# Moving the exchange of resident operands closer to their release in a Strassen-type matmul phase

## The reference

```python
def sq_relu_mlp(h, w1, w2):
    return jnp.square(jax.nn.relu(h @ w1)) @ w2

    x_lat = x_lat + m_lat[2] * y_lat          # y_lat ends in "@ w_out", 1024 x 1024
    h_lat = modulate(rms_norm(x_lat, norm2_g[l]), m_lat[3], m_lat[4])
    x_lat = x_lat + m_lat[5] * sq_relu_mlp(h_lat, w_mlp1[l], w_mlp2[l])   # 1024 x 4096, 4096 x 1024
return rms_norm(x_lat, final_g)
```

## Time and profile before

| | us |
|---|---|
| median of 3 runs | 3883.67 (3883.39 to 3904.89) |
| profiled execution, device time | 3888.39 |
| its span | 3886.6 |
| phase_out's products, first to last matmul | 2407.0 to 3873.8 |
| one f-unit or x-unit without exchange or turn | 19.04 |

### The profile page before, as it was taken

One profiled execution on the slowest core, in us unless ns is written; L12 is line 12 of the kernel. 1 busy time (PEld: TensorE's weight loads), 2 busy tenths in 40 slices (PEclk: granted clock), 3 DMA queues, 4 the chain that ended last, 5 costly groups with the idle time before them and its releaser, 6 DMA issues. The chain is left out here.

```text
span 3886.6 us, 98888 instructions
## 1 busy us (share of the span) xinstructions
PE 3376.4 (87%) x41417; PEld 2791.5 (72%) x41417; DVE 1966.0 (51%) x2884; ACT 1647.7 (42%) x2375; POOL 1668.3 (43%) x1364
## 2 busy tenths in 40 slices
PE   6899999999878888867777644989999999999998
PEld 3677888888767777756677513768877887777877
DVE  5488401110045555545555556564556546556575
ACT  5566313432145555532333412565555444323243
POOL 0220223222044545423555334545655665555554
PEclk7999999999989999985776766999999999999999
DMA  5133434453233333324343345676565557546453
GB/s 193 49 75 73 98 90 142 121 138 102 85 99 99 110 102 106 105 90 99 95 100 88 133 157 190 209 238 198 187 228 195 185 188 270 218 168 237 163 227 119
DMA packets 438927, 560.19 MB, mean 144 GB/s; under 512 B 119852, under 2 KB 355728, under 8 KB 413720
## 3 DMA queue, kind: packets, MB, share of 16 engines
q1 hardware_dynamic: 412704, 518.84, 41.8%
q10 hardware_dynamic: 20344, 21.04, 1.7%
q0 software_dynamic: 5632, 16.78, 1.5%
HBM read 354.42 MB, written 202.16 MB: 143 GB/s over the span
## 5 line engine op out<-in xcount | busy, mean ns | idle before, releaser
L2788 PE MATMUL o_pg<-o_t_hi,o_s_hi 128*128 128x512 f32 x2016 | 795.6, 395 | 62.7 <-DVE o_s_lo L2973 17.6
L2790 PE MATMUL o_pg<-o_t_lo,o_s_hi 128*128 128x512 f32 x2016 | 790.3, 392 | 0.0
L2791 PE MATMUL o_pg<-o_t_hi,o_s_lo 128*128 128x512 f32 x2016 | 789.8, 392 | 0.0
L601 PE MATMUL p_pg<-h_hi,p_whi 128*128 128x512 f32 (+1 forms) x1384 | 530.6, 383 | 9.6 <-DVE p_wlo L830 9.6
L601 PE MATMUL p_pg<-h_lo,p_whi 128*128 128x512 f32 (+1 forms) x1384 | 518.5, 375 | 0.0
L601 PE MATMUL p_pg<-h_hi,p_wlo 128*128 128x512 f32 (+1 forms) x1384 | 518.5, 375 | 0.0
L2788 PEld LDWEIGHTS o_pg<-o_t_hi,o_s_hi 128*128 128x128 f32 x2016 | 382.0, 189 | 157.8 <-issue 60.9
L2791 PEld LDWEIGHTS o_pg<-o_t_hi,o_s_lo 128*128 128x128 f32 x2016 | 381.9, 189 | 80.9
L2790 PEld LDWEIGHTS o_pg<-o_t_lo,o_s_hi 128*128 128x128 f32 x2016 | 382.5, 190 | 77.8
L2973 DVE TENSOR_TENSOR o_s_lo<-o_raw,o_s_hi 128x512 fp32r<-128x512 f32 x288 | 255.4, 887 | 209.3 <-ACT o_s_hi L2821 209.2
L601 PEld LDWEIGHTS p_pg<-h_hi,p_whi 128*128 128x128 f32 x1384 | 261.7, 189 | 61.0 <-DVE p_wlo L830 9.8
(11 more groups left out here) (330 smaller groups left out, 6625.1 us busy)
## 6 DMA issues: line engine op xcount, KB each, us to landing
o_raw<-in_w_mlp SPq DMA_DIRECT2D x32, 1024.0 KB, 5.9
scr_f<-o_xf SPq DMA_DIRECT2D x64, 512.0 KB, 7.7
o_raw<-scr_f SPq DMA_DIRECT2D x32, 1024.0 KB, 5.3
scr_w<-o_pre SPq DMA_DIRECT2D x16, 1792.0 KB, 6.5
o_t_raw<-scr_w SPq DMA_DIRECT2D x28, 1024.0 KB, 11.7
g_kqvb<-scr_kqv SPq DMA_DIRECT2D x72, 384.0 KB, 3.5
o_xf<-scr_x SPq DMA_DIRECT2D x22, 1024.0 KB, 7.9
p_raw<-in_w_in SPq DMA_DIRECT2D x38, 512.0 KB, 5.9
```

Of the source, the lines that this page charges most:

```text
L601: last = nc.tensor.matmul(pg[0:m, bank, 0:n], w[:, q, k, 0:m], h[bank][:, k, :], start=(k == 0 and j == 0), stop=(k == KT - 1 and j == 2))
L2788: nc.tensor.matmul(out, s_hi[:, q, k, :], t_hi[:, q, k, :], start=(not more and k == 0), stop=False, skip_group_check=more)
L2790: nc.tensor.matmul(out, s_hi[:, q, k, :], t_lo[:, q, k, :], start=False, stop=False, skip_group_check=more)
L2791: last = nc.tensor.matmul(out, s_lo[:, q, k, :], t_hi[:, q, k, :], start=False, stop=(k == 3), skip_group_check=more)
```

## The change

Eight edits in `phase_out`:

1. **Lag.** `T_HIGH` and `T_LOW` become 2 and 3: both splits of a resident part run one slot earlier in ScalarE's and VectorE's program. `prepared` and `LATE_PREP` say in which slot the next unit's stationary parts are prepared; with the values given each stays in its slot.
2. **Order of SyncE's queue at an exchange.** In the last unit `raw_load(i + 2)` stands ahead of `t_load` 0 instead of behind it. In the unit after, it moves to q = 1. For x-units the store of the unit before the last moves to q = 0 of the unit after, and the x tile that this unit needs is loaded one unit earlier (at q = 5 of the unit before the last). The x load of unit 40 moves from q = 2 to q = 5 of unit 39.
3. **Two turns by a diagonal.** For units 6 and 7 ScalarE doesn't scale x1 in place: it writes two 128 x 128 diagonals `diag` from the identity, and TensorE multiplies the unscaled tile by them (`matmul` in place of `transpose`). `scale` no longer waits for the store of x1, but for the turn before.
4. **`take_h(7)`** moves from slots (8, 5) and (8, 6) to (9, 2) and (9, 3).
5. **Joins.** For units 2 to 7, the pieces of the join of `h` move from two in slot 0 and two in slot 1 to one in slot 0, one in slot 1, two in slot 2. The last two joins move to slots 4 to 6 of units 8 and 9.
6. **`h_store`** moves from q = 2 to q = 3, for the last two blocks to q = 0 of units 9 and 10.
7. **`f_free`** waits for the store of x1 in the first two f-units.
8. The first load of `w_mlp2`'s preparation moves from slot 68 to slot 71.

```diff
--- before.py
+++ after.py
@@ -2297,10 +2297,11 @@
 UPB = 4
 PLAIN = {0: (0, 0), 2: (1, 0), 3: (0, 1), 5: (1, 1)}
 MIXED = {4: 0, 1: 1, 6: 2}
-PRE_AT = [68 + 13 * t for t in range(7)] + [171 + 13 * t for t in range(8)] + [281]
+PRE_AT = [71 + 13 * t for t in range(7)] + [171 + 13 * t for t in range(8)] + [281]
 PRE_PIECES = {3: (0, 1), 4: (2,), 5: (3, 4), 6: (5, 6), 7: (7,)}
 PRE_STORE = 9
-T_HIGH, T_LOW = 3, 4
+T_HIGH, T_LOW = 2, 3
+LATE_PREP = ((0,), (1,), (2,), (3,), (4,), (5,), (6,))
 
 
 def join_operands(eng, t, done, count):
@@ -2509,6 +2510,7 @@
         xf = sb("xf", [P, 2, 2 * D])
         pre = sb("pre", [P, 7, TB])
         ss, rs = sb("ss", [P, 2]), sb("rs", [P, 2])
+        diag = sb("diag", [P, 2, P])
         bank = ctx.enter_context(nc.psum_tensor("o_pg", [P, 4, TB], F32))
         pt = ctx.enter_context(nc.psum_tensor("o_pt", [P, 4, TB], F32))
         BX, BY, BV, BZ = range(4)
@@ -2532,6 +2534,14 @@
         N = M2 + FC * NW
         SETS = [0, M1, M1 + N1 // 2] + [M2 + NW * c for c in range(FC)]
         LAST_OF = {at - 1: k for k, at in enumerate(SETS) if k}
+
+        def prepared(i, q):
+
+            if i in LAST_OF:
+                return [(i + 1, q)]
+            if i - 1 in LAST_OF:
+                return [(i + 1, p) for p in LATE_PREP[q]]
+            return [(i + 1, q)] if i + 1 < N else []
 
         def is_x(i):
             return i < M1 or i >= M2
@@ -2672,20 +2682,29 @@
                 raw_load(1)
                 x_load(1)
                 for i in range(N + 2):
+                    last, first = i in LAST_OF, i - 1 in LAST_OF
                     for q in range(7):
-                        if i in LAST_OF:
+                        if q == (1 if first else 0) and i + 2 < N:
+                            raw_load(i + 2)
+                        if last:
                             t_load(LAST_OF[i], q)
-                        if q == 0:
-                            if i + 2 < N:
-                                raw_load(i + 2)
-                        if q == 1 and M1 <= i - 1 < N and not final_unit(i - 1):
+                        if q == 1 and M1 <= i - 1 < M2:
                             store(i - 1)
-                        if q == 2 and 0 <= i - 2 < M1:
+                        if not last and q == 1 and M2 <= i - 1 < N and not final_unit(i - 1):
+                            store(i - 1)
+                        if first and q == 0 and M2 <= i - 2:
+                            store(i - 2)
+                        if q == 3 and 0 <= i - 2 < M1 - 2:
                             h_store(i - 2)
+                        if q == 0 and M1 - 2 <= i - 3 < M1:
+                            h_store(i - 3)
                         if 7 * i + q - PRE_STORE in PRE_AT:
                             pre_store(PRE_AT.index(7 * i + q - PRE_STORE))
-                        if q == (5 if i + 1 == M2 + 2 else 2) and M2 <= i + 1 < N:
-                            x_load(i + 1)
+                        if M2 <= i + 1 < N and not (last and i >= M2):
+                            if q == (5 if i + 1 in (M2, M2 + 2) else 3 if first else 2):
+                                x_load(i + 1)
+                        if q == 5 and i + 1 in LAST_OF and i + 1 >= M2:
+                            x_load(i + 2)
                         if 7 * i + q in PRE_AT:
                             pre_load(PRE_AT.index(7 * i + q))
                         if q == 4 and final_unit(i - 1):
@@ -2798,8 +2817,11 @@
                         pe.wait_ge(h_taken, 8 * i)
                     for k in range(KT):
                         for m in range(2):
-                            last = nc.tensor.transpose(pt[:, k // 2, (k % 2 * 2 + m) * P:(k % 2 * 2 + m + 1) * P],
-                                                       x_tile(i)[:, m, k * P:(k + 1) * P], e.ident)
+                            to, tile = pt[:, k // 2, (k % 2 * 2 + m) * P:(k % 2 * 2 + m + 1) * P], x_tile(i)[:, m, k * P:(k + 1) * P]
+                            if i < M1 - 2:
+                                last = nc.tensor.transpose(to, tile, e.ident)
+                            else:
+                                last = nc.tensor.matmul(to, tile, diag[:, m, :], start=True, stop=True)
                     last.then_inc(turned, 1)
 
                 for i in range(N + 1):
@@ -2837,6 +2859,7 @@
                         eng.wait_ge(f_out[n % 2], 32 * (n // 2))
                     else:
                         eng.wait_ge(turned, NW - 1 + n)
+                        eng.wait_ge(x1_out[n], 16 * (NW // 2))
 
                 def rectify(i, k, src, to):
                     n = 3 * (i - M1) + k - 1
@@ -2879,6 +2902,11 @@
 
                 def scale(i):
                     act.wait_ge(inv, i + 1)
+                    if i >= M1 - 2:
+                        act.wait_ge(turned, i)
+                        for m in range(2):
+                            nc.scalar.activation(diag[:, m, :], e.ident, ACT.Copy, scale=rs[:, m:m + 1]).then_inc(scaled, 1)
+                        return
                     act.wait_ge(x1_out[i % 2], 16 * (i // 2 + 1))
                     for m in range(2):
                         t = x_tile(i)[:, m, :]
@@ -2907,8 +2935,8 @@
                                 take_p1(i)
                             if not is_x(i):
                                 f_unit(i, q)
-                        if i + 1 < N:
-                            s_high(i + 1, q)
+                        for at in prepared(i, q):
+                            s_high(*at)
                         if exchange(i, q, T_HIGH):
                             t_high(*exchange(i, q, T_HIGH))
                         if 0 <= i - 1 < M1 or final_unit(i - 1):
@@ -2921,8 +2949,10 @@
                         if 0 <= i - 1 < M1:
                             if q == 3:
                                 scale(i - 1)
-                            if q >= 5:
+                            if q >= 5 and i - 1 < M1 - 1:
                                 take_h(i - 1, q - 5)
+                        if i - 1 == M1 and 2 <= q <= 3:
+                            take_h(i - 2, q - 2)
 
             @block.vector
             def _(dve):
@@ -2932,6 +2962,7 @@
                         dve.wait_ge(f_out[n % 2], 32 * (n // 2))
                     else:
                         dve.wait_ge(turned, NW - 1 + n)
+                        dve.wait_ge(x1_out[n], 16 * (NW // 2))
 
                 def place(i, which):
 
@@ -2993,18 +3024,23 @@
                     for q in range(7):
                         if 0 <= i < N and q:
                             combine(i, q)
-                        if i + 1 < N:
-                            s_low(i + 1, q)
+                        for at in prepared(i, q):
+                            s_low(*at)
                         if exchange(i, q, T_LOW):
                             t_low(*exchange(i, q, T_LOW))
                         if (0 <= i - 1 < M1 or final_unit(i - 1)) and q == 2:
                             inverse(i - 1)
                         if final_unit(i - 1) and q == 3:
                             finish(i - 1)
-                        if 0 <= i - 2 < M1 and q < 2:
+                        if 0 <= i - 2 < M1 - 2 and q < 3:
                             if q == 0:
                                 dve.wait_ge(h_taken, 8 * (i - 1))
-                            for k in (2 * q, 2 * q + 1):
+                            for k in ((0,), (1,), (2, 3))[q]:
+                                join_piece(dve, lambda n: pre[:, n, :], k, h_joined, 4 * (i - 2))
+                        if M1 - 2 <= i - 2 < M1 and q >= 4:
+                            if q == 4:
+                                dve.wait_ge(h_taken, 8 * (i - 1))
+                            for k in ((0,), (1,), (2, 3))[q - 4]:
                                 join_piece(dve, lambda n: pre[:, n, :], k, h_joined, 4 * (i - 2))
 
 

```

## The result

The changed kernel takes 3900.07 us (median of 20 executions, 3891.26 to 3909.13), the kernel before 3888.04 (20, 3881.66 to 3904.89): a ratio of 1.0024, with a 95% interval of 1.0015 to 1.0033 (the two medians by themselves are 12.0 us apart, 1.0031, inside that interval). Medians here are of all executions of a kernel, ratios leave out those in which the chip was in a visibly slower state. The forecast was 3883, the range 3858 to 3900. The kernel is slower by a quarter of a per cent, which 20 executions of each can tell, and lies within 1%, as 0.95 of the chance said; but the forecast was no change, and the median stands just past the range's upper end. Some 4.4 of the 17.1 us between 3883 and 3900.07 are no part of the change: the forecast stood on a median of three executions, 3883.67, and 20 of the same kernel give 3888.04.

What follows compares the result with a forecast made beforehand. TensorE was taken as busiest, with 72.8 us of phase_out's losses to win and VectorE's order deciding the exchanges. The terms -4.2 - 8 + 3.7 + 3.7 + 2.9 + 1.8 = -0.1 gave 3883 us, range 3858 to 3900.

Steps and rivals of the forecast that it cites:

- units 7 and 8: Turns by the diagonal, without the wait for x1's store, and fewer join pieces ahead: -8 us, bounds -12 and -4.
- the price of the turn: Units 6 and 7: a float32 diagonal turn is no dearer than a transposition's 2.09 us; upper bound +2 each.
- Rival C: The float32 turns in units 7 and 8 cost 2 x 6.3 us more: 3895 us, chance 0.05.
- Joins: Units 2 to 6: one piece in slot 0 lets combine start earlier, 0.84 us a unit: -4.2, bounds -4.2 and 0.
- rival D: At the joins product 3 stays late because the smaller pieces still meet GpSimd: +4.2, 3888 us, chance 0.06.
- Unit 9: `take_h(7)` waits for block 6's store, TensorE loses 4.8 us, the earlier 1.13 go: +3.7, bounds -1 and +6.
- Exchanges 24 and 40: Part 0, behind the raw load, lands late and delays ScalarE and the combines: +3.7 at 24, +2.9 at 40.
- its upper bound: Exchanges 24 and 40: all the half clock, and `take_p1` behind the late `t_high`s: +5.6 us each.
- Exchanges 48 to 64: Five `t_low`s, not four, ahead of `combine(i, 1)` pay back the earlier slot: +0.4 to +0.6 each, +1.8 in sum.
- rival B: Parts late for slot 2 hold up ScalarE at all five exchanges, +5.6 us each: 3903 us, chance 0.17.
- Within 1%: The changed kernel's time lies within 1% of the kernel before: chance 0.95.
- rival A: The shorter lag pays: five exchanges each 2.72 us shorter, unit 9 wins 1.13: 3857 us, chance 0.22.

Runs made afterwards that it cites:

- after_lag34: The changed kernel with the lag alone set back to 3 and 4: 3886.46 us, ratio 0.9996 to the kernel before.
- after_part0_first: The changed kernel with `t_load` 0 ahead of `raw_load` again in the last unit before an exchange: 3893.83 us against 3889.33, ratio 1.0012.
- lag_only: The kernel before with the shorter lag (2 and 3) alone: 3895.25 us against 3889.33, ratio 1.0023.
- early_only: The changed kernel, old lag and old handling of h's last two blocks, first four parts' splits a slot earlier at 48, 56, 64: 3879.26 us beside 3891.74.
- best: As early_only, and the next unit's stationary parts prepared later at exchanges 48, 56 and 64: 3878.46 us against 3891.74, ratio 0.9971.
- the kernels that defer: Three kernels, best among them, that prepare the next unit's stationary parts later after exchanges; deferral alone, at every exchange: 3883.47 us against 3893.0.

## Why the prediction was wrong

**The account closes.** The step that failed above all is the one on units 7 and 8: the diagonal's turn taken as no dearer than a transposition, and priced as if it met the full clock. Undoing the lag in the changed kernel takes away 9.7 us, then undoing the move of the last two blocks 7.2 more; what is left, the joins, the diagonals and the queue's order, is a gain of 7.3 over before. 9.7 + 7.2 - 7.3 = 9.6. So a gain of the kind that the prediction saw was there, and two edits gave back more than it. Its size is less sure than the sum looks: 5.9 of the 7.3 lie in units 7 and 8 and are taken from the highest (61.9) of three traces that run from 57.7 to 61.9, and an edit's share depends on which others are in.

**Units 7 and 8: the step that failed, 6.7 us.** Up to the turn it held nearly: `t_high(0)` waited for part 0, the roots behind it, and `t_low(0)` ended at 2579.3 on before's time axis (3.83 subtracted), forecast 2578.5. Turn(6) was put at 2577.5 and began at 2579.3, 1.8 late, because part 1 was late too (ScalarE stood 1.83 us for it) and the prediction had let ScalarE wait for part 0 alone: the two parts landed 12.66 and 17.11 us into unit 7, 4.45 apart, where the price for the next MB was 2.45. Then its price was taken as 2.1 at most, and it was 6.51. So product (7, 5) ended at 2592.40, on before's axis at 2588.6, where the forecast's own times give 2582.3, and VectorE, said to run without a gap, stood 4.80 us for it. Product (8, 3) started at 2604.0 on that axis, 5.3 later than forecast; what stands behind it, turn(7) at 3.73 above all, added 1.4. The wrong terms are the price of the turn, the clock behind the gap of 5.39, which the prediction had priced in the exchanges and not here, and the wait for part 1. The prediction had said what would show it wrong, and this did: 16 matmuls that take far over 2.1 us. Most of the -8 needs the old lag: after_lag34 has -5.8.

**The price of a float32 matmul.** The earlier trace rows was misread. Its 64 records are 32 calls, each recorded twice, and their stationary operand is 64 columns wide: 116 ns a call, not 58. At 128 wide the diagonal's call takes 3.73 / 16 = 233 ns, against 1.97 / 16 = 123 for a transposition; a turn costs 1.76 more at full clock, and 2.8 more in the two half-clock pairs (6.51 against 3.68). The code of the line would have told it: it has two loops that make 32 calls. The upper bound of +2 a turn held for the full clock alone. Rival C, with a chance of 0.05, was right in kind and had 6.3 for 1.8. The sentence of the Trainium skill (TensorE: Matmul & The Clock Gate, Terms), that its transpose mode is 4 times faster for float32, has the right sign; this trace shows a factor of 1.9 between the two turns at full clock.

**Joins: -2.2, not -4.2, a term mis-sized.** Edit 5 works, in every kernel that has it; rival D is what half of it met. In units 3, 4 and 5 product 2 still takes 3.13 us with the wait behind it, not 2.72, since the piece in slot 0 starts late there, 6.04 us into the unit, behind an `s_low` that is late or takes up to 1.5; in units 2 and 6 it starts at 4.7 and 4.9. The piece itself takes 1.78 us in all five, the second one 0.68. Units 2 and 6 lose nothing (21.13); units 3, 4 and 5 lose 0.5, 0.5 and 1.0.

**Unit 9: right, and too small.** `take_h(7)` was released 15.05 us into the unit, forecast 14.5, by the transfer named. TensorE's stalls in units 9 and 10 were 7.0, not 4.8, since unit 10's products 1 and 2 took 2.5 longer, for `take_p1` and the combine behind it.

**Exchanges 24 and 40: right in place, too large.** ScalarE stood 2.47 us for part 0 in unit 23, as named; `combine(24, 1)` came 39.02 us after unit 23's start against 34.97 before, +4.05 where +4.5 was said, and product 3 within 0.3 of its forecast. From there the prediction charged 1 us of half clock to products 3 to 5; the slow matmuls lay in product 2 (5.14), and unit 25 lost 0.64 less. TensorE's long wait there is one that the prediction kept for its upper bound: product 2 stands 7.53 us for `take_p1(24)`, and product 3 only 0.54 for the combine.

```profile
2933.44 0.76 PE L2807 MATMUL o_pg<-o_t_hi,o_s_hi 128*128 128x512 f32 x1 [7.53 <-ACT o_part L2854]
```

Nor is VectorE without a gap in these exchanges, as the prediction said of all five: between the first `t_low` and `combine(24, 1)` or `combine(40, 1)` it stood 3.8 us in sum in the kernel before, 5.6 and 6.6 in the changed one. after_part0_first shows the cause of the loss, part 0 behind the raw load: -1.5 and -1.9 without it.

**Exchanges 48 to 64: right in mechanism.** Five `t_low`s ahead of `combine(i, 1)`, +0.6 at 48 (+1.2 was said), and less lost behind it (product 6 has no wait of its own any more). Part 0 had too little slack at 56 and 64: `combine(56, 1)` and `combine(64, 1)` came 1.1 and 0.8 later than unit 48's, rival B's mechanism at a fraction of its 5.6. lag_only shows that without the queue's new order the lag costs 2.0 to 2.6 each, mostly through late parts.

**The chances.** "Within 1%" was right, and rival A, at 0.22, had the sign wrong in units 9 and 10 and at every exchange but the first behind 48 (-0.3 for its -2.7). The range's upper end, 3900, was cut where half of B and all of C had been spent; that two edits of the same sign could miss together (turn and take_h) was in no case.

## What to carry to other kernels

Before a wait is moved earlier on an in-order engine, list what it now stands ahead of: the short lag brought no operand sooner than its transfer, but put two waits for DMA ahead of the roots and the diagonal, and a fifth `t_low` ahead of the combine that the next product needs. When an in-order engine has no gap, whoever waits for one of its results gains only if work that stood ahead of that result is put behind it, which is what early_only and best show. When an operation of another kind replaces one, count its records against its calls in the trace, and look for a row with the same width on both sides.

## What the runs showed of the hardware

A float32 matmul of 128 x 128 by 128 columns appears as two records and takes 233 ns at full clock; the transposition of the same tile is one record and takes 123 (3.73 us and 1.97 us for 16). A float32r matmul of a product has 512 columns and takes 227 ns (2.72 us for 12), so plain float32 costs about four times as much for each column. Turns by the diagonal took 3.73 or 3.84 us at a granted clock of 1.00, and 6.37 to 6.51 behind a gap of 5.4 to 5.6, with 0.58 and 0.57 recorded. Outside the loading of the first set, `t_low` takes 2.27 to 2.29 us or 3.34 to 3.40, save 18 of 2.6 to 2.8 in the kernels that defer. Which one is a matter of who began first: each of the longer ones has a GpSimd operation that had begun some 0.4 us or more before it, while 61 in which a GpSimd operation began 0.16 us behind them took 2.28 like those alone. The start of phase_out moves by 18 us between profiled executions of kernels that are alike up to it, more than any edit here is worth: a phase has to be compared by its own length.
